# Seven block products for two more pairs of input projections in a hybrid attention and retention layer

## The reference

```
h   = RMSNorm_pre(x)
z   = h @ w_in            # 1024 x 5632, split into qa, ka, va (512 each), qr, kr, vr, gr (512 each), ga, gb (1024 each)
s   = qa . kb * dh**-0.5 + table[:, clip(dist, -128, 128) + 128]     # banded attention with learned position bias
A   = softmax(s) . vb
R   = retention(qr, kr, vr), head group norm, swish gate
mix = (sigmoid(ga) * (A @ w_attn_out) + sigmoid(gb) * (R @ w_ret_out)) @ w_o
x   = x + RMSNorm_post(mix)
x   = x + RMSNorm_post(relu(RMSNorm_pre(x) @ w_ff_up)**2 @ w_ff_down)
```

## Time and profile before

| | us |
|---|---|
| median of 3 runs | 864.88 (864.26 to 864.89) |
| the profiled execution's own time | 864.71 |
| its span, first to last instruction | 862.9 |
| PE busy in the span | 848.0 (98%) |
| DVE busy | 560.8 (65%) |
| ACT busy | 353.3 (41%) |
| POOL busy | 18.5 (2%) |

### The profile page before, as it was taken

How to read it: one execution, slowest core, us unless ns; L and a number is a source line. 1 busy time by engine, 2 the same in 40 slices (tenths; PEclk the granted TensorE clock), 3 DMA queues, 4 the chain that set the end, 5 groups by cost and what they waited for, 6 DMA issues and landing times.

```text
span 862.9 us, 16613 instructions
## 1 busy us (share of the span) xinstructions
PE 848.0 (98%) x6714; PEld 829.5 (96%) x6714; DVE 560.8 (65%) x977; ACT 353.3 (41%) x565; POOL 18.5 (2%) x26
## 2 busy tenths in 40 slices
PE   8999999999989999999999999999999999999996
PEld 7999999999979999999999999999999999999996
DVE  6323788888868667666436765897633773267545
ACT  6211466666551111254446454434411451145442
POOL 1000000000000000000100000000000000000000
PEclk9999999999999999999999999999999999999999
DMA  9333225233332213122341132132323123312403
GB/s 307 101 98 97 76 68 129 78 72 95 81 100 75 85 55 96 59 78 69 98 147 51 50 99 98 49 98 97 99 97 97 51 95 97 97 52 95 147 1 104
DMA packets 79172, 78.51 MB, mean 91 GB/s; under 512 B 3360, under 2 KB 76208, under 8 KB 79120
## 3 DMA queue, kind: packets, MB, share of 16 engines
q1 hardware_dynamic: 68784, 70.39, 25.3%
q10 hardware_dynamic: 9360, 5.25, 2.7%
q0 software_dynamic: 976, 2.14, 1.2%
HBM read 72.75 MB, written 5.01 MB: 90 GB/s over the span
## 4 chain that ended last, share of the span: by engine, by line
PE 88%; DVE 5%; ACT 3%; issue 2%; DMA 2%; ACTq 0%; SPq 0%; DVEq 0%
PE acc L969 62%; PE wk L969 3%; PE wk L993 2%; PE wk L1395 2%; PE wk L1393 2%; PE wk L1394 2%; PE acc L1042 1%; PE wk L1287 1%; PE acc L1287 1%; PE acc L1288 1%; PE wk L1288 1%; PE wk L1289 1%; PE acc L1289 1%; DMA x_nat<-in_x_prompt 1%; ACT w_hi L495 1%
## 5 line engine op out<-in xcount | busy, mean ns | idle before, releaser
L495 ACT ACTIVATE w_hi<-w_raw 128x1024 fp32r<-128x1024 f32 x103 | 109.2, 1060 | 293.1 <-PE acc L969 266.0
L969 PE MATMUL acc<-act_hi,w_hi 128*128 128x272 f32 x992 | 209.1, 292 | 0.0
L969 PE MATMUL acc<-act_hi,w_lo 128*128 128x272 f32 x992 | 205.3, 288 | 0.0
L969 PE MATMUL acc<-act_lo,w_hi 128*128 128x272 f32 x992 | 204.7, 288 | 0.0
L969 PEld LDWEIGHTS acc<-act_hi,w_hi 128*128 128x128 f32 x992 | 155.8, 188 | 4.2 <-issue 0.8
L969 PEld LDWEIGHTS acc<-act_lo,w_hi 128*128 128x128 f32 x992 | 155.8, 188 | 0.0
L969 PEld LDWEIGHTS acc<-act_hi,w_lo 128*128 128x128 f32 x992 | 155.0, 189 | 0.0
L1505 DVE TENSOR_TENSOR w_lo<-w_raw,w_hi 128x1024 fp32r<-128x1024 f32 x103 | 126.0, 1223 | 28.6 <-ACT w_hi L495 27.5
L969 PE MATMUL acc<-mid_hi,w_hi 128*128 128x272 f32 x544 | 112.7, 288 | 0.4
L969 PE MATMUL acc<-mid_hi,w_lo 128*128 128x272 f32 x544 | 111.9, 288 | 0.0
L969 PE MATMUL acc<-mid_lo,w_hi 128*128 128x272 f32 x544 | 111.7, 287 | 0.0
(11 more groups left out here) (327 smaller groups left out, 1363.8 us busy)
## 6 DMA issues: line engine op xcount, KB each, us to landing
w_raw<-in_w_in SPq DMA_DIRECT2D x43, 512.0 KB, 4.5
w_raw<-in_w_ff_up SPq DMA_DIRECT2D x32, 512.0 KB, 4.3
...
```

Source lines behind the costliest of these rows:

```text
L495: act.activation(w_hi[:, v % 2], w_raw[:, v // 2, :, P * (v % 2):P * (v % 2) + P], ACT.Copy).then_inc(hi_ready, 1)
L969: ins = pe.matmul(dst[:, n, 0:HALF], w[:, k, :], h[:, k, HALF * n:HALF * n + HALF], start=begin, stop=end)
```

## The change

Groups 1 and 2 use the seven products for their tiles 2 and 3. The helpers of the feed-forward part become common ones (`seven` on PE, `seven_high` on ACT, `seven_low` on DVE); the loops over the two groups are written out. The mixed token blocks of the first norm (`early_sums`, `early_hi`, `early_lo`) lie in memory that attention uses later. They are made in group 0. The position bias is formed between groups 0 and 1, on PE and on DVE, since its products and the seven results both use `wk`. In `z` the last two tiles of such a group are summed up first and then multiplied by `rstd` (`normed`). The counts of the shared semaphores in the feed-forward part are shifted.

```diff
+        early_at = first + arena_bytes - 4 * 2 * 4 * (KT // 2) * HALF
+        early_sums = place("early_sums", [P, 4, KT // 2, HALF], at=early_at)
+        early_lo = place("early_lo", [P, 4, KT // 2, HALF], fr, at=early_at)
+        early_hi = place("early_hi", [P, 4, KT // 2, HALF], fr, at=ends["early_lo"])
+        early_out = place("early_out", [P, 3, HALF], at=ends["x_waste"])
+        assert ends["early_hi"] <= first + arena_bytes and ends["early_out"] <= early_at
...
+            def seven_high(g, u, first_out, tile_done=lambda j: None):
+                act.wait_ge(mm_done, 4 * g + 1)
+                act.wait_ge(w_in_sem[1], 32 * (g + 1))
+                unit_high(0, BLOCK_11).then_inc(unit_hi, 1)
+                act.wait_ge(unit_sum, 11 * u + 3)
+                unit_high(1, w_sum_2[:]).then_inc(unit_hi, 1)
+                tile_done(0)
+                act.wait_ge(mm_done, 4 * g + 2)
+                act.activation(w_hi[:, 1], w_sum_31[:].rearrange("p s k c -> p (s k) c"), ACT.Copy).then_inc(unit_hi, 1)
+                tile_done(1)
+                act.wait_ge(unit_done, 6 * u + 1)
+                act.activation(first_out, UNIT_DST[0], ACT.Copy).then_inc(out_1_ready, 1)
...
+            def mixed_scale(sums, norm, r, k):
+                m, n = ((0, 0), (4, 1), (0, 1), (4, 0))[r]
+                act.activation(sums[:, r, k, :], xT[:, m + k, HALF * n:HALF * n + HALF], ACT.Copy, scale=gains[:, norm, m + k:m + k + 1])\
+                    .then_inc(mixed_scaled, 1)
+            def mixed_high(sums, to, r, added):
+                act.wait_ge(mixed_added, added)
+                act.activation(to[:, r], sums[:, r], ACT.Copy).then_inc(mixed_rounded, 1)
...
+            for r in range(3):
+                for k in range(4):
+                    mixed_scale(early_sums, 0, r, k)
             split_ahead(0, 1)
             act.wait_ge(kc_tr, 1)
             act.activation(kcT[:], wk[:].rearrange("p (a b) -> p a b", a=PAIRS), ACT.Copy).then_inc(kc_ready, 1)
+            for k in range(4):
+                mixed_scale(early_sums, 0, 3, k)
             split_ahead(0, 2)
+            for r in (1, 2, 0, 3):
+                mixed_high(early_sums, early_hi, r, 4)
             split_ahead(0, 3)
...
-            with act.Fori(1, G_RET) as g:
-                for j in range(4):
-                    split_ahead(g, j)
+            for g in range(1, G_RET):
+                seven_high(g, g - 1, early_out[:, 0])
...
             column_tile(0, 3, act_hi, act_lo)
-            with pe.Fori(1, G_RET) as g:
-                for j in range(4):
-                    column_tile(g, j, act_hi, act_lo)
-
-
             pe.wait_ge(hankel_in, 16)
             pe.wait_ge(const_in, 32)
...
+            def unit(dst, n, hi, lo):
+                for k in range(KT // 2):
+                    pe.matmul(dst, slot(w_hi, n)[:, k, :], hi[:, k, :], start=k == 0, stop=False)
+                    pe.matmul(dst, slot(w_hi, n)[:, k, :], lo[:, k, :], start=False, stop=False)
+                    ins = pe.matmul(dst, slot(w_lo, n)[:, k, :], hi[:, k, :], start=False, stop=k == KT // 2 - 1)
+                return ins
...
+            def seven(g, u, hi, lo, made):
+                column_tile(g, 0, act_hi, act_lo)
+                column_tile(g, 1, act_hi, act_lo)
+                mixed = [(hi[:, r], lo[:, r]) for r in range(4)]
+                if made == 1:
+                    pe.wait_ge(bias_ready, 1)
+                pe.wait_ge(unit_lo, 5 * u + 1)
+                unit(UNIT_DST[0], 0, *plain(0, 0)).then_inc(unit_done, 1)
+                pe.wait_ge(mixed_ready, made)
+                pe.wait_ge(unit_lo, 5 * u + 2)
+                unit(UNIT_DST[1], 1, *mixed[1]).then_inc(unit_done, 1)
+                pe.wait_ge(unit_lo, 5 * u + 3)
+                unit(UNIT_DST[2], 2, *mixed[2]).then_inc(unit_done, 1)
+                unit(UNIT_DST[3], 3, *mixed[0]).then_inc(unit_done, 1)
+                pe.wait_ge(unit_lo, 5 * u + 4)
+                unit(UNIT_DST[4], 0, *plain(1, 0)).then_inc(unit_done, 1)
+                pe.wait_ge(unit_lo, 5 * u + 5)
+                unit(UNIT_DST[5], 2, *plain(1, 1)).then_inc(unit_done, 1)
+                pe.wait_ge(lo_ready, 4 * g + 4)
+                pe.wait_ge(unit_sum, 11 * u + 5)
+                unit(UNIT_DST[1], 3, *mixed[3]).then_inc(mm_done, 2)
+            for g in range(1, G_RET):
+                seven(g, g - 1, early_hi, early_lo, 1)
...
-            with dve.Fori(0, G_RET) as g:
-                for j in range(4):
-                    to_z(g, j, 4 * g + j)
-                    split_ahead(g, j)
+            def seven_low(g, u, outs, dst, evacuate, finished, tile_done=lambda j: None, dst_free=lambda: None):
...
+                dve.wait_ge(w_in_sem[1], 32 * (g + 1))
+                summed(w_sum_31[:, 0], BLOCK_11, BLOCK_21, 1)
+                summed(w_sum_31[:, 1], BLOCK_22, BLOCK_21, 2)
+                evacuate(0)
+                summed(w_sum_2[:], w_sum_31[:, 1], BLOCK_11, 3)
+                summed(w_sum_4[:], w_sum_2[:], BLOCK_12, 4)
+                unit_low(0, BLOCK_11, 1).then_inc(unit_lo, 1)
+                unit_low(1, w_sum_2[:], 2).then_inc(unit_lo, 1)
+                tile_done(0)
+                evacuate(1)
+                dve.wait_ge(unit_hi, 5 * u + 3)
+                dve.tensor_tensor(w_lo[:, 1], w_sum_31[:].rearrange("p s k c -> p (s k) c"), w_hi[:, 1].bitcast(fp), ALU.subtract).then_inc(unit_lo, 1)
+                unit_low(0, BLOCK_12, 4).then_inc(unit_lo, 1)
...
+            def mixed_add(sums, scaled_count):
+                a, b, c, d = (sums[:, n] for n in range(4))
+                dve.wait_ge(mixed_scaled, scaled_count)
+                order.after(dve.tensor_tensor(a, a, c, ALU.subtract))
+                order.after(dve.tensor_tensor(c, b, c, ALU.subtract))
+                order.after(dve.scalar_tensor_tensor(b, b, -1.0, a, ALU.mult, ALU.subtract))
+                dve.scalar_tensor_tensor(d, b, -1.0, d, ALU.mult, ALU.subtract).then_inc(mixed_added, 4)
+            def mixed_low(sums, hi, to, r, rounded):
+                dve.wait_ge(mixed_rounded, rounded)
+                return dve.tensor_tensor(to[:, r], sums[:, r], hi[:, r].bitcast(fp), ALU.subtract)
+            for j in range(4):
+                to_z(0, j, j)
+                split_ahead(0, j)
+                if j == 2:
+                    mixed_add(early_sums, 16)
+            for n, r in enumerate((1, 2, 0, 3)):
+                ins = mixed_low(early_sums, early_hi, early_lo, r, n + 1)
+            ins.then_inc(mixed_ready, 1)
             dve.wait_ge(bias_mm, 1)
             order.after(dve.tensor_tensor(bias[:], wk[:].rearrange("p (h c) -> p h c", h=AH),
...
             dve.memset(bias[0:AD, :, P + AD:2 * P], NEG).then_inc(bias_ready, 1)
             order.flatten()
...
+            for g in range(1, G_RET):
+                def normed(j):
+                    row = z[:, 4 * g + 2 + j, :]
+                    if j == 0:
+                        return dve.tensor_tensor(row, row, rstd[:], ALU.mult)
+                    return dve.scalar_tensor_tensor(row, row, -1.0, rstd[:], ALU.mult, ALU.mult)
+                seven_low(g, g - 1, tuple(early_out[:, n] for n in range(3)), (z[:, 4 * g + 2, :], z[:, 4 * g + 3, :]),
+                          lambda j: to_z(g, j, 4 * g + j), normed)
```

More of the change, by code:

```diff
@@ L339, in strassen @@
         def strassen(c, i):
-            return 2 * c + i - 2
+            return 2 * c + i
         def halves(ap):
@@ L1568, in _, with summed, unit_low @@
             order.flatten()
-            with dve.Fori(0, G_RET) as g:
-                for j in range(4):
-                    to_z(g, j, 4 * g + j)
-                    split_ahead(g, j)
+            def seven_low(g, u, outs, dst, evacuate, finished, tile_done=lambda j: None, dst_free=lambda: None):
+                one, two, three = outs
+                def summed(out, a, b, n):
+                    dve.tensor_tensor(out, a, b, ALU.add).then_inc(unit_sum, 1)
+                    dve.wait_ge(unit_sum, 11 * u + n)
+                def unit_low(n, block, ready):
+                    dve.wait_ge(unit_hi, 5 * u + ready)
+                    return dve.tensor_tensor(slot(w_lo, n), block, slot(w_hi, n).bitcast(fp), ALU.subtract)
+                dve.wait_ge(w_in_sem[1], 32 * (g + 1))
[11 more added lines that the diff above has]
+                unit_low(0, BLOCK_12, 4).then_inc(unit_lo, 1)
+                dve.wait_ge(out_1_ready, u + 1)
+                dve.wait_ge(unit_done, 6 * u + 2)
+                summed(two, one, UNIT_DST[1], 5)
+                dve.wait_ge(unit_done, 6 * u + 3)
+                summed(three, two, UNIT_DST[2], 6)
+                unit_low(2, w_sum_4[:], 5).then_inc(unit_lo, 1)
+                dve.wait_ge(unit_done, 6 * u + 4)
+                dst_free()
+                summed(two, two, UNIT_DST[3], 7)
+                summed(dst[1][:, HALF:T], three, UNIT_DST[3], 8)
+                dve.wait_ge(hi_ready, 4 * g + 4)
```

(23 more changed lines are left out.)

146 lines of the change are left out of this document (29 added, 117 removed).

## The result

The changed kernel takes 868.52 us (median of 6 runs, 867.82 to 870.55), beside 864.73 us (863.93 to 866.46) for the kernel before on the same chip: ratio 1.0048 with a 95% interval from 1.0035 to 1.0060, 0.5% slower. On a second chip it took 867.65 against 865.03 (1.0026, 1.0015 to 1.0037). The profiled execution took 867.82, with a span of 865.7.

The account below looks back on a forecast made before the run. PE, busy for 98% of the 862.9 us span, was taken to bound the kernel. Matmuls removed -2.95, wait +4.8 and attention's start +0.4 gave +2.25, so 867.0 us, with a range from 864.7 to 869.4.

Parts of the forecast that it names:

- rival A: Behind PE's new wait before group 1's first block product, clock also drops, losing about 2.05 us: 869.1; chance 0.25.
- the sum of +2.25: Whole kernel: -2.95 for matmuls, +4.8 for the wait, +0.4 at attention's start, added to the profiled execution's 864.71.
- Matmuls removed: PE, groups 1 and 2: 12 matmuls fewer a group save 1.48 us each, -2.95 us for both.
- Bias products and scalings: Bias products moved before group 1 on PE, and scalings in ACT's idle stretch, cost 0.
- The line to PE's first block product: Group 1: DVE and ACT's queued work readies the first block's weights at 61.5, so PE waits +4.8 us.
- The start of attention: DVE's and ACT's line to the first probabilities falls later against PE: +0.4 us, between 0 and 0.9.
- Rival C: At PE's 2.2 us `p_lo` wait, something keeping its time, such as a load, gives delay back: 864.8; chance 0.13.
- the prediction's own signs of being wrong: First-block idle under 4.0 or over 6.1 us, PE also waiting for tile (1,1), or a shrinking `p_lo` wait.
- Rival B: Groups 1 and 2: new work fits DVE's and ACT's idle time, so PE gains 2.95 us: 861.9; chance 0.10.

Follow-up runs that it names:

- e3_woven: As e2, with the mixed blocks' four low parts on DVE spread out and a PE wait for each block by itself; 861.25 us, ratio 0.9968.
- e2: Changed kernel with bias and corner formed on DVE before the low part of tile (1,1) instead of later; 863.35 us, ratio 0.9988.
- e1: Changed kernel with 16 needless 128-column PE products in the wait before group 1's first block product; 867.54 us, ratio 1.0038.
- e4: Kernel before, with only the position bias formed behind group 0 on PE and DVE, plain products throughout; 865.08 us, ratio 0.9997.
- e5: As e3_woven, with ACT loading the exponential's table before the last rounding of group 2 instead of after it; 860.93 us, ratio 0.9960.
- after_again: The changed kernel, unchanged, run again on a second chip; 867.65 us, ratio 1.0026 to the kernel before.
- e7: Changed kernel with seven products in group 2 alone, group 1 plain, bias formed before the low part of tile (1,1); 862.22 us, ratio 0.9972.
- e1_again: e1 run again, on the chip of after_again; 866.40 us, ratio 1.0018.
- e8: Kernel before, with ScalarE's two stores of the last pair's keys moved from ahead of the rope load to behind the last stacking of probabilities; 870.63 us, ratio 1.0070.
- e9: As e5, with the same move of the two stores as in e8; 869.02 us, ratio 1.0050.
- e2_again: e2 run again unchanged, on the same chip as e7_again; 863.34 us, ratio 0.9989.
- e7_again: e7 run again unchanged, on the same chip as e2_again; 863.65 us, ratio 0.9992.

## Why the prediction came out as it did

The median of 868.52 lies inside the range, 1.5 above the forecast; the forecast's own range (866.2 to 868.0) misses it, and rival A's 869.1 is nearer (to the second chip's 867.65 the forecast is). In the profiled execution the sum of +2.25 stands against +3.11. Four of the six runs have a mean granted clock of 0.994, the profiled one 0.997, so part of what they take beyond it may be clock as well; no trace shows where. Term by term:

- **Matmuls removed, -2.95.** Right. 24 rows are gone, and group 2 takes 22.57 (73.67 to 96.24), as the feed-forward pair. `e3_woven` shows the gain whole once the wait is gone.
- **Bias products and scalings, 0.** Right: 41.55 for the products; the scalings cost no wait before the first tile.
- **The line to PE's first block product, +4.8.** 4.40 (from 57.15 to 61.55). The pieces stand where they were put: bias at 54.38 (said: near 54), first weight sum at 57.24 (57.05), products released at 61.55 (61.5). The 0.4 is from both ends: PE came 0.45 later than said (57.15 for 56.7), 0.33 of it by its inputs, while DVE's line began 0.24 later (37.97 for 37.73) and made it up on its last piece, from the first weight sum to the end of the first low part (4.16 for 4.43). `e2` and `e3` show the mechanism by taking the idle time away in two steps: 4.23, 1.44, none. It was one price too little, though: the same wait also costs clock.
- **Rival A, the idle PE loses clock, +2.05 with a chance of 0.25.** This is the step that failed: the forecast took the clock as unchanged behind the wait, and it fell in both profiles of this kernel (0.54 and 0.61 in the two windows behind it, and 0.50 and 0.72). Its size was 1.57 and 1.49, since the slow stretch was 3.4 us and not the 4.1 of the warm-up. My argument against it, that the clock row shows 9 in every slice of before, was a reading error: a slice is 21.6 us, and the row of after, with the dip in it, shows 9 in every slice too. Only narrow windows, or the distance of like matmuls, show such a loss, and at the very start only the distance: there the 18 rows of before are 0.227 apart where the bias products are 0.109 apart, yet its window from 2 to 4 us reads 1.00. The Trainium skill's "TensorE: Matmul & The Clock Gate", "HAM oscillation — how this bites in real kernels", had it right: a wait of this length brings the lower clock back; the trace agrees (4.23 us idle, then 0.54), and `e1` shows that PE work in the wait prevents it. The waits in that section's example are longer than the 1.80 us behind which the clock fell here too (the table at the end).
- **The start of attention, +0.4.** 0.47 (0.53 to 1.00). `e4` has it without the rest, `e5` takes most of it away by moving the table load.
- **Rival C, the delay given back at `p_lo`, -2.2 with a chance of 0.13.** It came in part, beside A. In this profile 1.03 is given back, in that of `after_again` 2.02 (PE is 3.95 later at the first probabilities, 113.23 to 117.18, and 1.93 later at the last weighted values, 244.33 to 246.26). One of the prediction's own signs of being wrong is there with it: the wait at `p_lo` shrank, from 2.20 to 1.70 and 0.68. I read the wait as DVE's work on PE's own transposes, which would move along. DVE in fact stood in a wait for `rope_sb`:

```profile
235.99 0.52 ACTq L670 DMA_DIRECT2D out_new_k_sample<-k_nat  x1
236.56 0.44 ACTq L725 DMA_DIRECT2D rope_sb<-in_rope  x1
243.55 1.45 DVE L1821 TENSOR_TENSOR rope_tmp<-z,rope_sb 64x544 f32<-64x544 f32 x2 [2.48 <-DMA rope_sb<-in_rope]
```

In the changed kernel's profile PE is 3.82 later but the load is issued only 1.47 later (235.09 to 236.56), because the small store ahead of it took 0.52 to issue instead of 2.87; the load then took 6.99 from issue to use instead of 5.67. 1.47 + 1.32 = 2.79, just the shift of the weighted values. It is not a fixed event that swallows a delay. The load's time differs between executions of one kernel (6.99 here, 5.97 in `after_again`); the issue's time did not in this place, so the short issue may belong to the change (below).
- **Rival B, faster, 861.9, 0.10.** Not this kernel, but `e3_woven` is what it described: DVE's work in its idle time. The reason given against it, the fixed order on DVE, was the true one.

So the +3.11 is the sum of +2.25 with six differences: the clock +1.57, the inputs +0.33, 0.31 outside the span and 0.07 at the probabilities, less the part given back, 1.03, and 0.40 of the wait. The two large ones, neither of them in the sum, have opposite signs. That the number came this near is partly luck; the wait and the matmuls removed are not.

## What to carry to other kernels

When an engine near 100% gets a new wait, price the clock behind it too, and look at the granted clock in windows of about 2 us; the page's slices hide it. Before taking saved matmuls as a gain, write down the other engine's queue up to the first operand that they need, and put the work with a later reader behind it: here the order on VectorE, with PE's waits split to match, made 868 or 861 out of the same operations. Before moving a store later, look for every wait on its landing, and not only for who overwrites its source.

## What the runs showed beyond that

**The clock after an idle of PE.** All are single places in a trace; the cost is the time to the next like landmark against a trace with full clock.

| idle of PE, us | where | granted clock behind it | cost, us |
|---|---|---|---|
| 0.49, 0.51, 0.68, 0.88 | `p_lo` in e7, e1_again, after_again, e8 | full | 0 |
| 1.16, 1.28, 1.34, 1.43 | `p_lo` in e9, e1_busy_wait, e5, e2_again | full | 0 |
| 1.44, 1.45 | first product in e2, e2_again | full | 0 |
| 1.70, 1.85, 2.20 | `p_lo` in after, e3, before | full | 0 |
| 1.80, 1.80, 2.17 | `p_lo` in e2, e7_again, e4 | 0.56, 0.50, 0.68 | 1.45, 2.80, 1.45 |
| 4.23, 4.23 | first product, after, after_again | 0.54, 0.50 | 1.57, 1.49 |
| 3.74, 3.90 | `z` in e8, e9 | 0.52, 0.53 | 4.07, 4.45 |

Between 1.8 and 2.2 us it went either way, and behind similar idles the slow stretch was 3 us or 9. What decides it is open. Of the three costs behind 1.80 and 2.17 us a later wait of 0.8 at `z` gives a part back: at the products behind it 0.5, 2.0 and 0.4 are left. It is likely a source of scatter too: of the 23 runs of the kernel before on the last chip, the three slowest (866.57 to 867.01) have the three lowest mean clocks (0.994 to 0.995). `e4`'s profile has such a dip (two windows of 0.68 and 0.50 behind 2.17 us), and the 0.4 that it costs is as much as the half us that was looked for.

**Issue and landing of a DMA.** The store of 16 KB `out_new_k_sample` takes ScalarE's queue 0.52 us to issue in 43 of its 56 places in fourteen traces, but 2.87 before the `rope_sb` load in the kernel before and 2.95 there in `e4`; in `e8`, where it no longer stands there, the load of `decay_sb` took 2.23 at the same time (0.45 in `e9`). These three are the kernels without the new products; in the other eleven traces no issue there took more than 0.52. Where a kernel was traced twice, this store is slow to issue in the same places: 3.36 and 3.05 at 160.7 in `e1_busy_wait` and `e1_again`, 0.78 and 1.30 at 194.7 in the two of `e7`, nowhere in the two of the changed kernel and of `e2`. So a long issue looks like a thing of the kernel's timing and not of chance; what holds the queue is not shown. The landing is another matter: from its issue to its first use `rope_sb` (544 KB) took 5.65 to 7.13 us in fourteen traces, 5.78 and 7.10 in the two of `e7`. Since that kernel was the same, such a difference (1.3 us at the wait, more with the clock) is no effect of a change; it took a second profile to see that.
